# Hidden rows regrouped by DMA and turned by VectorE in 32x32 squares, instead of TensorE transposes, in seven experts of a two-layer trunk

## The reference, cut to what matters

```python
logits = xt @ w_router;  top_logit, top_e = top_k(logits, 2);  gate = softmax(top_logit)
y[rows of e] = (silu(x_e @ w_gate[e]) * (x_e @ w_up[e])) @ w_down[e]      # e = 0..7, hidden width 3584
out = layer_norm(ALPHA * x + sum over the two experts of gate * y)
```

## Time and profile before

| | |
|---|---|
| median of 3 runs | 1403.9 us (1403.68 to 1404.87) |
| the profiled execution | 1404.42 us, span 1402.6 us |
| PE busy | 1382.1 us, 99% of the span |
| DVE / ACT / POOL busy | 1122.0 / 958.9 / 40.2 us |
| DMA | 444.77 MB, mean 317 GB/s |
| granted TensorE clock | 0.997 |

### The profile page before, as it was taken

The page is one execution under the profiler, slowest core; times in us unless marked ns, Lnnn a source line. Parts: engine busy times, 40 slices in busy tenths (PEclk is TensorE's granted clock), DMA queues, the critical chain, the costliest instruction groups (busy, mean ns, idle before and its releaser), DMA issues.

```text
span 1402.6 us, 18857 instructions
## 1 busy us (share of the span) xinstructions
PE 1382.1 (99%) x6998; PEld 1162.5 (83%) x6998; DVE 1122.0 (80%) x993; ACT 958.9 (68%) x892; POOL 40.2 (3%) x51
## 2 busy tenths in 40 slices
PE   9999999999999999999999999999999999999996
PEld 8988888889888888888888888888888888888874
DVE  5647555574668888888888888988888888889997
ACT  6655544455657777777777777777777777778774
POOL 1200000000002000000000000000000000000200
PEclk9999999999999999999999999999999999999998
DMA  9834555535158999999999999999999999999950
GB/s 364 356 119 182 211 180 180 187 144 200 41 211 336 424 420 421 423 422 388 378 376 377 369 403 369 368 402 382 380 364 386 377 374 396 370 372 374 391 236 32
DMA packets 64930, 444.77 MB, mean 317 GB/s; under 512 B 7464, under 2 KB 7744, under 8 KB 13424
## 3 DMA queue, kind: packets, MB, share of 16 engines
q1 hardware_dynamic: 60192, 425.96, 77.8%
q0 software_dynamic: 4544, 18.07, 3.4%
q10 hardware_dynamic: 144, 0.07, 0.0%
HBM read 431.48 MB, written 12.59 MB: 317 GB/s over the span
## 4 chain that ended last, share of the span: by engine, by line
PE 91%; DVE 5%; ACT 2%; DMA 1%; issue 1%; SPq 0%; DVEq 0%; ACTq 0%
PE ps L555 26%; PE ps L557 25%; PE ps L556 25%; PE ps L614 6%; PE ps L615 3%; PE ps L1004 2%; DVE wlo L1425 2%; DMA raw<-w_dense 1%; ACT whi L1098 1%; ACT raw L1154 1%; PE ps L767 1%; PE ps L709 1%; DVE raw L1460 1%; PE ps L584 0%; PE ps L962 0%
## 5 line engine op out<-in xcount | busy, mean ns | idle before, releaser
L1425 DVE TENSOR_TENSOR wlo<-raw,whi 128x2048 fp32r<-128x2048 f32 x396 | 905.1, 2291 | 182.5 <-ACT whi L1098 181.2
L1098 ACT ACTIVATE whi<-raw 128x2048 fp32r<-128x2048 f32 x397 | 760.3, 1918 | 239.8 <-PE ps L557 233.1
L555 PE MATMUL ps<-whi,xt 128*128 128x512 f32 (+1 forms) x1096 | 432.9, 395 | 2.8 <-DVE wlo L1425 1.7
L557 PE MATMUL ps<-whi,xt 128*128 128x512 f32 (+1 forms) x1096 | 425.8, 389 | 0.0
L556 PE MATMUL ps<-wlo,xt 128*128 128x512 f32 (+1 forms) x1096 | 425.2, 388 | 0.0
L555 PEld LDWEIGHTS ps<-whi,xt 128*128 128x128 f32 x1096 | 205.9, 188 | 48.5 <-DVE wlo L1425 6.7
L557 PEld LDWEIGHTS ps<-whi,xt 128*128 128x128 f32 x1096 | 205.8, 188 | 43.3
L556 PEld LDWEIGHTS ps<-wlo,xt 128*128 128x128 f32 x1096 | 206.1, 188 | 40.0
L555 PE MATMUL ps<-whi,hth 128*128 128x512 f32 x464 | 181.7, 392 | 0.5 <-DVE wlo L1425 0.5
L557 PE MATMUL ps<-whi,htl 128*128 128x512 f32 x464 | 180.9, 390 | 0.0
L556 PE MATMUL ps<-wlo,hth 128*128 128x512 f32 x464 | 180.6, 389 | 0.0
(11 more groups left out here) (258 smaller groups left out, 837.6 us busy)
## 6 DMA issues: line engine op xcount, KB each, us to landing
raw<-w_moe SPq DMA_DIRECT2D x336, 1024.0 KB, 7.3
raw<-w_dense SPq DMA_DIRECT2D x61, 1024.0 KB, 4.8
x_slots<-hth POOLq DMA_DIRECT2D x16, 256.0 KB, 13.1
raw<-vec_rows POOLq DMA_DIRECT2D x4, 1024.0 KB, 7.1
y_rows<-work SPq DMA_DIRECT2D x8, 512.0 KB, 8.7
biasb<-x_slots POOLq DMA_DIRECT2D x7, 512.0 KB, 8.1
raw<-w_dense SPq DMA_DIRECT2D x4, 512.0 KB, 6.9
x<-x_in SPq DMA_DIRECT2D x2, 512.0 KB, 5.4
```

The source lines that it names most:

```text
L555: mm(o, lh, rh, start=start, stop=False)
L557: return mm(o, ll, rh, start=False, stop=stop)
L1098: A(unit(whi, j), raw[:, slot * UNIT:(slot + 1) * UNIT], ACT.Copy).then_inc(hi_rdy, 1)
L1425: dve.tensor_tensor(unit(wlo, j), raw[:, slot * UNIT:(slot + 1) * UNIT], unit(whi, j).bitcast(F32), ALU.subtract).then_inc(lo_rdy, 1)
```

## The change

Six of the seven hidden blocks of experts 0 to 6 are no longer transposed by PE. ACT's silu and DVE's product write the block with its columns in another order, into one of two row tiles (`h_rows`, by the parity of c). ACT then issues 16 DMAs from SBUF to SBUF (`hidden_move`), each of 32 partitions by 128 elements (16 KB), which put the 4x4 pieces of the block where they belong. DVE turns all 32x32 squares of the block in one instruction (`hidden_squares`), ACT makes the high part from that, now from SBUF, and POOL the low part. `EXP_ORDER` puts the down units of block c two blocks later instead of one, and there are two pairs of tiles for the parts, by the parity of c. With U the step of the second up unit, the DMAs stand at U+1, the squares at U+5 and the high part at U+6.

The token rows are treated alike: POOL writes them to DRAM with their columns regrouped (two copies into `acc` first), fetches them with four DMAs instead of one, and DVE turns them in two instructions into PSUM (`rows_turned`) at steps 31 and 32. Block 6 of these experts, and all of expert 7, still go through PE, with the down units in the new order.

```diff
     EXP_ORDER += [("gate", _c, 0), ("gate", _c, 1), ("up", _c, 0), ("up", _c, 1)]
-    if _c:
-        EXP_ORDER += [("down", _c - 1, 0), ("down", _c - 1, 1)]
-EXP_ORDER += [("down", EC - 1, 0), ("down", EC - 1, 1)]
+    if _c > 1:
+        EXP_ORDER += [("down", _c - 2, 0), ("down", _c - 2, 1)]
+for _c in (EC - 2, EC - 1):
+    EXP_ORDER += [("down", _c, 0), ("down", _c, 1)]
+
+MOVED = EC - 1
+UP_END = [EXP_ORDER.index(("up", _c, 1)) for _c in range(EC)]
+MOVE_AT = {UP_END[_c] + 1: _c for _c in range(MOVED)}
+SQUARES_AT = {UP_END[_c] + 5: _c for _c in range(MOVED)}
+HIDDEN_AT = {UP_END[_c] + 6: _c for _c in range(MOVED)}
...
 TAIL_BANKS = (7, 4, 0, 2)
+ROWS_TURN = (PER_EXP - 11, PER_EXP - 10)
 PICK_AT = (26, 29, 32, 35)
...
         def expert_hidden(c, f):
-            if c < EC - 1:
+            if c < EC - 1 and c % 2 == 0:
                 return hth[:, f * P:(f + 1) * P], htl[:, f * P:(f + 1) * P]
-            return xth[:, f, P:TOK], xtl[:, f, P:TOK]
+            f0 = 4 if c < EC - 1 else 0
+            return xth[:, f0 + f, P:TOK], xtl[:, f0 + f, P:TOK]
         def expert_hidden_all(c):
-            if c < EC - 1:
+            if c < EC - 1 and c % 2 == 0:
                 return [t[:, :].rearrange("p (k n) -> p k n", k=4) for t in (hth, htl)]
-            return [t[:, 0:4, P:TOK] for t in (xth, xtl)]
+            f0 = 4 if c < EC - 1 else 0
+            return [t[:, f0:f0 + 4, P:TOK] for t in (xth, xtl)]
+
+        h_rows = [htmp[:, :], spare[:, 512:1024]]
+        h_moved = [spare[:, 1024:1536], spare[:, 1536:2048]]
+        h_turned = [acc[:, 0, 0:512], acc[:, 0, 512:1024]]
...
             pool.wait_ge(slots_zero, 2 * N_EXP * 16)
-            pool.wait_ge(src_rdy, 8)
+            for tb in range(TB):
+                pool.wait_ge(src_rdy, 7 + tb)
+                pool.tensor_copy(acc[:, tb, :].rearrange("p (q k r) -> p q k r", q=4, k=KT),
+                                 x[:, tb, :].rearrange("p (k q r) -> p q k r", q=4, k=KT)).then_inc(x_perm, 1)
+            pool.wait_ge(x_perm, TB)
             pool.wait_ge(x_to_rdy, 1)
...
                                         out_offset=bass.IndirectOffsetOnAxis(ap=x_to[:, i:i + 1], axis=0),
-                                        in_=x[:, i // 2, :], in_offset=None,
+                                        in_=acc[:, i // 2, :], in_offset=None,
                                         bounds_check=N_EXP * P - 1, oob_is_err=False).then_inc(x_put, 16)
...
                 pool.wait_ge(ga_ps, n)
-                pool.dma_start(xg, x_slots[n * P:(n + 1) * P, :]).then_inc(ga_in, 16)
+                for q in range(4):
+                    pool.dma_start(xg[32 * q:32 * q + 32, :].rearrange("s (u c) -> s u c", u=4),
+                                   x_slots[n * P:(n + 1) * P, 256 * q:256 * q + 256].rearrange(
+                                       "(u s) c -> s u c", u=4)).then_inc(ga_in, 16)
+                for c in range(MOVED):
+                    h, l = expert_hidden_all(c)
+                    pool.wait_ge(m_hi, (n - 1) * EC + c + 1)
+                    pool.tensor_tensor(l, h_turned[c % 2].rearrange("p (k n) -> p k n", k=4), h.bitcast(F32),
+                                       ALU.subtract).then_inc(m_lo, 1)
             pool.wait_ge(pick_rdy, 1)
...
-                pe.wait_ge(ga_in, n * 16)
+                pe.wait_ge(ga_in, n * 16 + 48 * (N_EXP - 1))
                 for kt in range(KT):
...
                         find_rows(e + 1)
-                    if (what, half) == ("gate", 1) and c:
+                    if (what, half) == ("gate", 1) and c and (last or again):
                         hidden_t(c - 1)
-                    if j == PER_EXP - 4:
+                    if j == PER_EXP - 5:
                         hidden_t(EC - 1)
-                    if j == PER_EXP - 3 and not last:
+                    if j == PER_EXP - 3 and again:
                         turn_rows(e + 1)
...
-            def gated(e, j, c):
+            def gated(e, j, c, moved):
                 act.wait_ge(w_used, e * PER_EXP + (N_DENSE + j + 1))
-                A(htmp[:, :], ps[c % 2][:, :], ACT.Silu).then_inc(m_silu, 1)
-
-            def hidden_hi(e, c):
+                if moved:
+                    A(h_rows[c % 2].rearrange("p (q f r) -> p f q r", q=4, f=4),
+                      ps[c % 2][:, :].rearrange("p (f q r) -> p f q r", q=4, f=4), ACT.Silu).then_inc(m_silu, 1)
+                else:
+                    A(htmp[:, :], ps[c % 2][:, :], ACT.Silu).then_inc(m_silu, 1)
+
+            def hidden_hi(e, c, moved=False):
                 act.wait_ge(m_tr, e * EC + (c + 1))
-                A(expert_hidden_all(c)[0], ps[4][:, :].rearrange("p (k n) -> p k n", k=4), ACT.Copy).then_inc(m_hi, 1)
+                A(expert_hidden_all(c)[0], (h_turned[c % 2] if moved else ps[4][:, :]).rearrange("p (k n) -> p k n", k=4),
+                  ACT.Copy).then_inc(m_hi, 1)
+
+            def hidden_move(e, c):
+
+                act.wait_ge(m_h, e * EC + (c + 1))
+                for q in range(4):
+                    for u in range(4):
+                        act.dma_start(h_moved[c % 2][32 * q:32 * q + 32, P * u:P * u + P],
+                                      h_rows[c % 2][32 * u:32 * u + 32, P * q:P * q + P]).then_inc(h_in[c % 2], 16)
...
                     if (what, half, c) == ("up", 1, EC - 1):
-                        gated(e, j, c)
-                    if j == PER_EXP - 4:
+                        gated(e, j, c, False)
+                    if j == PER_EXP - 5:
                         hidden_hi(e, EC - 1)
...
                     if (what, half) == ("up", 1) and c < EC - 1:
-                        gated(e, j, c)
-                    if (what, half) == ("gate", 1) and c:
+                        gated(e, j, c, not (last or again))
+                    if (what, half) == ("gate", 1) and c and (last or again):
                         hidden_hi(e, c - 1)
+                    if j in MOVE_AT and not (last or again):
+                        hidden_move(e, MOVE_AT[j])
+                    if j in HIDDEN_AT and not (last or again):
+                        hidden_hi(e, HIDDEN_AT[j], True)
                     if j == PER_EXP - 3 and not last:
...
+            def rows_turned(n, half):
+
+                if half == 0:
+                    dve.wait_ge(ga_in, n * 64)
+                else:
+                    dve.wait_ge(m_h, n * EC - 1)
+                r = dve.transpose(ps[1 + 2 * half][:, :].rearrange("p (k u s) -> p k u s", k=4, u=4),
+                                  xg.rearrange("p (u k r) -> p k u r", u=4, k=KT)[:, 4 * half:4 * half + 4])
+                if half == 1:
+                    r.then_inc(ga_ps, 1)
+
             def scattered(n, tb):
...
-            def gated(e, c):
+            def gated(e, c, moved):
                 dve.wait_ge(m_silu, e * EC + (c + 1))
-                dve.tensor_tensor(htmp[:, :], htmp[:, :], ps[2 + c % 2][:, :], ALU.mult).then_inc(m_h, 1)
-
-            def hidden_lo(e, c):
+                if moved:
+                    h = h_rows[c % 2].rearrange("p (q f r) -> p f q r", q=4, f=4)
+                    dve.tensor_tensor(h, h, ps[2 + c % 2][:, :].rearrange("p (f q r) -> p f q r", q=4, f=4),
+                                      ALU.mult).then_inc(m_h, 1)
+                else:
+                    dve.tensor_tensor(htmp[:, :], htmp[:, :], ps[2 + c % 2][:, :], ALU.mult).then_inc(m_h, 1)
+
+            def hidden_squares(e, c):
+
+                dve.wait_ge(h_in[c % 2], e * (256 * MOVED // 2) + 256 * (c // 2 + 1))
+                if c == 0:
+                    dve.wait_ge(x_put, 16 * 2 * TB)
+                if c > 1:
+                    dve.wait_ge(m_lo, e * EC + (c - 1))
+                dve.transpose(h_turned[c % 2].rearrange("p (f u s) -> p f u s", f=4, u=4),
+                              h_moved[c % 2].rearrange("p (u f r) -> p f u r", f=4, u=4)).then_inc(m_tr, 1)
+
+            def hidden_lo(e, c, after_moved=False):
                 dve.wait_ge(m_hi, e * EC + (c + 1))
+                if after_moved:
+                    dve.wait_ge(m_lo, e * EC + MOVED)
                 h, l = expert_hidden_all(c)
...
                     if (what, half, c) == ("up", 1, EC - 1):
-                        gated(e, c)
-                    if j == PER_EXP - 4:
-                        hidden_lo(e, EC - 1)
+                        gated(e, c, False)
+                    if j == PER_EXP - 5:
+                        hidden_lo(e, EC - 1, not (last or again))
                     if j == PER_EXP - 1 and (last or again):
...
                     if (what, half) == ("up", 1) and c < EC - 1:
-                        gated(e, c)
+                        gated(e, c, not (last or again))
+                    if j in SQUARES_AT and not (last or again):
+                        hidden_squares(e, SQUARES_AT[j])
+                    if j in ROWS_TURN and not (last or again):
+                        rows_turned(e + 1, ROWS_TURN.index(j))
```

(2 more changed lines are left out.)

## The result

The changed kernel takes **1826.1 us** (median of 4 runs, 1825.81 to 1835.07) against 1403.8 us before: a ratio of 1.302, 95% interval 1.299 to 1.306. The prediction said 1583 us, 1500 to 1655. It had the direction; the size was off by 243 us, beyond the range.

A forecast was written before the change was run, and what follows sets the result against it. PE, busy 99%, was taken as the bound. Per round, -3.5 us of transposes, +28.6 of stops and +0.4 of delayed low parts make +25.5; seven rounds add 178.5 to 1404.4, giving 1583 us, range 1500 to 1655.

The forecast's parts named there:

- What bounds the kernel, and the mechanism: PE bounds the expert loop; ACT's 16 issues delay its next high part, stopping PE 4.45 to 5.0 us per block.
- 96a-7.9: PE's stops per round in us, summed over blocks 0 to 5, for issue price a; 28.6 us at 0.38.
- the price of one issue, a: Time ACT's queue needs per DMA issue: 0.38 us, a lone issue plus 0.05 between issues; bounds 0.33 and 0.48.
- I count every matmul at the present pace: PE's matmuls in the loop keep clock 1.00; a lower clock would prove the prediction wrong, with no size given.
- POOL's low part: Low parts of six hidden blocks on POOL, 1.27 us each, in time for every block; block 0's has 0.4 us to spare.
- the sentence that stood beside the sum: If POOL's subtraction waits for DVE's low part, block 0's part ends 1.2 us late each round; total about 1591 us.
- The squares at 0.68: DVE's turn of a hidden block's 32x32 squares takes 0.68 us, between limits of 0.6 and 2.29.
- The DMA landing at nothing: DVE's squares wait at no cost for the DMAs, with 2.6 us of cover; late-landing rival near 1738 us, chance 0.08.
- The cheap issue (1380): Rival: an issue on ACT costs under 0.1 us, all removed transposes are gained, 1380 us; chance 0.07.
- An issue of 0.29: Upper end of the rival that small pieces issue in 0.12 to 0.29 us: 1407 to 1526 us; chance 0.12.
- 0.48 with the waiting low part: Upper case: issue price 0.48 us, 1650 us alone, plus POOL's low part waiting for DVE's; counted inside the range to 1655.

The follow-up runs named there:

- experiment 1: Changed kernel with one DMA of the whole tile per block instead of sixteen, pieces not regrouped; 1384.1 us, ratio 0.986 to the kernel before the change.
- experiment 3: Changed kernel with the hidden blocks' low parts made on DVE instead of POOL, same issues; 1814.0 us, ratio 1.293 to the kernel before the change.
- experiments 4, 5 and 8: Against the changed kernel, in turn: issues on SP's queue, 1507.2 us; four at a time on ACT, squares of blocks 1-4 a step later, 1518.6; through DRAM on SP's queue, 1586.2.

## Why the prediction was right and wrong

- **What bounds the kernel, and the mechanism: right.** The issues stand between the high parts of U+1 and U+2, the next high part is held until the last issue, and PE stops once per block with 1.1 to 1.6 us of slack against the burst. With 0.64 us for one issue the prediction's own formula, 96a-7.9, gives 53.5 us of stops a round, 375 over seven. Measured: 350.
- **The step that failed: "the price of one issue, a".** It was put at 0.38 with 0.33 and 0.48 as bounds. Measured: 0.51 us for the first, 0.61 for each behind it, 0.64 from start to start. The bounds came from rows of another kind: 1 MB from HBM on SP, a few at a time. None moved SBUF to SBUF, and none came as the fifteenth in a row. The sentence that "2 packets per DMA engine should not hold the next issue up as 8 do" chose a value inside the bounds by an argument without a row, and pointed the wrong way. One DMA of 128 partitions from SBUF to SBUF took 0.472 (experiment 1), and the small piece takes more, not less: 0.51 when it stands first, 0.61 behind another. Why one behind another is held longer stays open. By the formula this term alone is worth 7 x 96 x (0.64-0.38) = 175 us of the 243.
- **"I count every matmul at the present pace": the term that was missing.** The text named the clock among what would prove it wrong, but gave it no price. It is worth 95 us of busy time (experiment 1 against the changed kernel). Against the sum the stops came out 25 us shorter than the formula. 1583 + 175 + 95 - 25 is 1828.
- **POOL's low part: in time by the sum, late in fact.** It takes 2.4 to 2.9 us instead of 1.27, because it waits for DVE's, and ends PE's wait in one block of each round. In the stop shown it ended 1.13 us behind the low part that PE would else have waited for; the sentence that stood beside the sum had 1.2 and a price of 8 us. Measured, 12 us (experiment 3). That rule should have stood in the sum.
- **The squares at 0.68: right** (0.705). **The DMA landing at nothing: right here only.** Its cover was the stop itself: the prediction had said that stops thin the weight traffic, and 266 GB/s came where it had been 383 (600 to 1200 us). In experiments 4, 5 and 8, which took most of the stops away, the late landing became the bound.
- **The rivals.** The cheap issue (1380) described experiment 1's time within 4 us, but needed a price of 0.1. The Trainium skill, DMA: Bandwidth & Descriptors, section "Anatomy of one DMA — SWDGE (gpsimd) path", gives about 50 ns for the dispatch, on POOL's path; what the queue of ACT or SP is held for here is twelve times that. No rival had an issue dearer than the dearest row, and that is where the result lay.
- **Two small sums don't come out.** An issue of 0.29 gives 1522 us by the formula, not 1526, and 0.48 with the waiting low part 1658, 3 above the range. Neither matters here.

## What to carry to other kernels

Before a step is replaced by many small DMAs, multiply their number by the issue time of exactly that shape, measured in a burst: here 16 x 0.64 us stood in the order of an engine with 1.1 us to spare. Issues placed just behind an instruction that the engine has been handed run beside it; issues placed ahead of one hold it. And a transfer that lands in time while the kernel is stopped has to be costed again for the kernel without stops, with the weights at full rate.

## What the runs showed of the hardware

- An issue of 32 partitions by 512 bytes, SBUF to SBUF, takes 0.61 us in a burst, on ACT's queue and nearly the same on SP's (0.59); one of 128 partitions by 2 KB takes 0.47, and a 1 MB load 0.33.
- PE resumed at 1.2 GHz (granted clock 0.50) after the two stops of 8 us shown and stayed there for 3 and 6; its busy time grew almost as much with stops of 3 us (88 against 95 us).
- VectorE turns 128x512 fp32 values in squares of 32 in 0.705 us, near the 0.684 of its subtraction of that size.
- A subtraction on POOL with both inputs in SBUF waits for the end of a low part of DVE that started before it: it takes 2.4 to 3.1 us in the changed kernel, of which 1.13 to 1.17 lie behind that end, and 1.27 otherwise. DVE's next low part waits for POOL's end in its turn, 3.25 us instead of 2.29.
- Four issues on ACT's queue, 2.45 us, ran beside a high part of ACT that had been passed on just before.
